# Expert weights by halves of the contraction, one queue for all loads, and a hinted jump

## The reference, cut to what matters

```python
for e in range(N_EXPERTS):
    h = jax.nn.silu(t @ w1[e]) * (t @ w3[e])
    y = y + combine[:, e:e + 1] * (h @ w2[e])
```

## Time and profile before

| | |
|---|---|
| median of the runs | 752.1 us |
| the profiled execution's own time | 756.08 us |
| its span, first to last instruction | 753.9 us |
| TensorE busy (matmul) | 665.2 us, 88% |
| VectorE, ScalarE busy | 220.6 us, 171.4 us |
| mean granted TensorE clock | 0.948 |
| read from HBM | 228.23 MB, 304 GB/s over the span |
| first MoE stage, pair 0 to pair 7 | 144.5 to 366.5 us |
| second MoE stage | 519.9 to 741.8 us |

### The profile page before, as it was taken

The page is one execution under the profiler, slowest core; times in us unless marked ns, Lnnn a source line. Parts: engine busy times, 40 slices in busy tenths (PEclk is TensorE's granted clock), DMA queues, the critical chain, the costliest instruction groups (busy, mean ns, idle before and its releaser), DMA issues.

```text
span 753.9 us, 7800 instructions
## 1 busy us (share of the span) xinstructions
PE 665.2 (88%) x2948; PEld 293.7 (39%) x2948; DVE 220.6 (29%) x628; ACT 171.4 (23%) x380; POOL 17.9 (2%) x29
## 2 busy tenths in 40 slices
PE   5997999899999979995589877999999999799864
PEld 2444544533434323331144444455343343243221
DVE  2367812420222110210224588124202220112102
ACT  2015712212220220210401366022112202202101
POOL 2000000000000000000001021000000000000000
PEclk9997999999999998998979979997999999989988
DMA  9999534489999999999999346642999999999951
GB/s 275 276 280 394 203 109 166 177 325 399 392 396 391 398 395 392 399 389 397 295 263 333 142 105 206 228 177 109 360 399 393 396 392 396 397 389 399 391 207 57
DMA packets 94392, 229.70 MB, mean 305 GB/s; under 512 B 2363, under 2 KB 2443, under 8 KB 94364
## 3 DMA queue, kind: packets, MB, share of 16 engines
q1 hardware_dynamic: 85184, 195.08, 72.4%
q10 hardware_dynamic: 7612, 29.74, 10.0%
q0 software_dynamic: 1568, 4.50, 2.5%
HBM read 228.23 MB, written 1.08 MB: 304 GB/s over the span
## 4 chain that ended last, share of the span: by engine, by line
DMA 44%; PE 43%; DVE 7%; issue 3%; ACT 1%; SPq 1%; DVEq 0%; ACTq 0%
DMA attw<-in_w_dram 23%; DMA ring<-in_w_dram 19%; PE ps L881 11%; PE ps L1044 9%; PE ps L954 7%; PE ps L1068 5%; PE ps L1014 2%; PE ps L1025 2%; DMA attw<-in_w_qkv_dram 2%; PE ps L918 1%; PE ps L932 1%; DVE attw L641 1%; PE ps L945 1%; DVE attw L626 1%; PE ps L996 1%
## 5 line engine op out<-in xcount | busy, mean ns | idle before, releaser
L1044 PE MATMUL ps<-attw,work 128*64 128x512 f32 x512 | 120.5, 628 | 28.8 <-DMA attw<-in_w_dram 28.8
L1068 PE MATMUL ps<-ring,work 128*64 128x512 f32 x384 | 114.3, 595 | 2.9 <-ACT work L485 2.9
L1044 PE MATMUL ps<-ring,work 128*64 128x512 f32 x512 | 111.6, 594 | 0.0
L881 PE MATMUL ps<-attw,work 128*128 128x512 f32 x192 | 87.1, 614 | 0.5 <-DMA attw<-in_w_qkv_dram 0.5
L757 DVE TENSOR_TENSOR work<-work,ps 128x512 f32<-128x512 f32 x16 | 11.0, 688 | 249.8 <-PE ps L1044 249.8
L1044 PEld LDWEIGHTS ps<-attw,work 128*64 128x64 f32 x512 | 40.6, 145 | 107.6 <-issue 107.6
L494 ACT COPY work<-ps 32x512 f32<-32x512 f32 x64 | 36.9, 577 | 132.0 <-PE ps L1068 131.5
L1044 PEld LDWEIGHTS ps<-ring,work 128*64 128x64 f32 x512 | 37.8, 137 | 67.8 <-issue 66.8
L766 DVE COPY work<-ps 32x512 f32<-32x512 f32 x64 | 43.9, 686 | 59.9 <-PE ps L1068 59.3
L1068 PE MATMUL ps<-attw,work 128*64 128x512 f32 x128 | 57.6, 595 | 0.6 <-ACT work L485 0.6
L954 PE MATMUL ps<-attw,work 128*128 128x512 f32 x128 | 56.3, 595 | 0.0
(11 more groups left out here) (133 smaller groups left out, 483.2 us busy)
## 6 DMA issues: line engine op xcount, KB each, us to landing
ring<-in_w_dram SPq DMA_DIRECT2D x42, 2048.0 KB, 16.7
attw<-in_w_dram SPq DMA_DIRECT2D x40, 2048.0 KB, 16.0
ring<-in_w_dram ACTq DMA_DIRECT2D x14, 2048.0 KB, 12.6
attw<-in_w_qkv_dram SPq DMA_DIRECT2D x4, 2048.0 KB, 16.7
attw<-in_w_o_dram SPq DMA_DIRECT2D x8, 1024.0 KB, 20.6
attw<-in_w_qkv_dram SPq DMA_DIRECT2D x4, 1024.0 KB, 15.0
attw<-bias_rows POOLq DMA_DIRECT2D x8, 256.0 KB, 3.6
x_sb<-in_x_dram SPq DMA_DIRECT2D x2, 512.0 KB, 5.9
```

What stands on the lines that cost most here:

```text
L881: last = pe.matmul(ps[:, g, :], xT[:, k, P * tt:P * tt + P], wqkv[part][:, k, :], start=(k == 0), stop=(k == KB - 1))
L1044: last = pe.matmul(ps[64 * e:64 * e + 64, 6 + which, :], xg[:, k, c:c + 2 * SLOTS], w13(which, e)[:, k, :], start=(k == 0), stop=(k == KB ...
L1068: last = pe.matmul(ps[64 * e:64 * e + 64, 4 + half, :], hT[:, k, 64 * e:64 * e + 64], w2(e)[:, k, 512 * half:512 * half + 512], start=(k = ...
```

## The change

A unit now is a half of the contraction of one matrix for both experts of a pair (blocks 0 to 3 and 4 to 7 of w1 and w3, 0 and 1, 2 and 3 of w2), loaded by two DMAs of 1 MB, one for each expert. TensorE waits for a unit where its half begins and signals behind each half (`w13_used` counts four a pair). w2 runs half by half of the contraction: both halves of the columns with unit 4, and then both with unit 5; `w2_used` now counts three a pair, one behind unit 4 and one behind each half of columns with unit 5. The waits for landings in `load_over` are gone. Unit 5 of pair i+1 is issued by SP, behind unit 4 of pair i+2. TensorE reads the flag ahead of the last pair, and its branch over the extra rounds is hinted from there. The other engines jump as before.

```diff
-        def ring_w13(which, e):
-            return ring[:, 2 * which + e, :].rearrange("p (k f) -> p k f", k=KB)
+        def w13_view(unit):
+            return unit.rearrange("p (e k f) -> p e k f", e=2, k=KB // 2)
+        def w2_view(unit):
+            return unit.rearrange("p (e k f) -> p e k f", e=2, k=FB // 2)
+        def ring_w13(which, kh):
+            return w13_view(ring[:, 2 * which + kh, :])
...
-        w1v = w1.rearrange("l e (k p) f -> l e p k f", p=P)
+        w1v = w1.rearrange("l (q e) (h k p) f -> l q h e p k f", e=2, h=2, p=P)
...
-                sp.dma_start(dst, view[L, 2 * pair + u % 2]).then_inc(landed, 16)
+                for e in range(2):
+                    sp.dma_start(dst[:, e], view[L, pair, u % 2, e]).then_inc(landed, 16)
...
-            def load_over(L, i, load_pair, mine, others, done, others_done):
-                n = PAIRS * L + i + 1
-                sp.wait_ge(main.w1_used, n)
+            def load_over(L, i, load_pair):
+                n = PAIRS * L + i
+                sp.wait_ge(main.w13_used, 4 * n + 1)
                 load_pair(L, i + 2, (0,))
-                sp.wait_ge(others[4], others_done)
+                sp.wait_ge(main.w13_used, 4 * n + 2)
                 load_pair(L, i + 2, (1,))
-                sp.wait_ge(main.w3_used, n)
+                sp.wait_ge(main.w13_used, 4 * n + 3)
                 load_pair(L, i + 2, (2,))
-                sp.wait_ge(mine[1], done)
+                sp.wait_ge(main.w13_used, 4 * n + 4)
                 load_pair(L, i + 2, (3,))
-                sp.wait_ge(main.w2_used, 2 * n)
+                sp.wait_ge(main.w2_used, 3 * n + 1)
                 load_pair(L, i + 2, (4,))
+                sp.wait_ge(main.w2_used, 3 * n + 3)
+                load_unit(L, i + 1, 5, last_landed)
...
+                sp.wait_ge(main.w2_used, 3 * (n - 1))
+                load_unit(L, PAIRS - 1, 5, last_landed)
                 if L + 1 < DEPTH:
-                    sp.wait_ge(main.w1_used, n)
+                    sp.wait_ge(main.w13_used, 4 * n - 3)
                     load_wqkv(L + 1, 0)
+                    sp.wait_ge(main.w13_used, 4 * n - 2)
                     load_wqkv(L + 1, 1)
-                    sp.wait_ge(main.w3_used, n)
+                    sp.wait_ge(main.w13_used, 4 * n - 1)
                     load_wqkv(L + 1, 2)
-                    load_wo(L + 1, 0)
-                    sp.wait_ge(main.w2_used, 2 * n)
-                    load_wo(L + 1, 1)
+                    sp.wait_ge(main.w13_used, 4 * n)
+                    sp.wait_ge(main.w2_used, 3 * n - 2)
+                    for a in range(2):
+                        load_wo(L + 1, a)
...
-                    if load_last:
-                        act.dma_start(ring_w2(1), w2v[L, 2 * (i + 1) + 1]).then_inc(last_landed, 16)
...
-                    landed(4)
-                    landed(5)
-                    for half in range(2):
-                        for k in range(FB):
+                    def down(kh, half):
+                        for k in range(2 * kh, 2 * kh + 2):
...
+                    landed(4)
+                    down(0, 0)
+                    pe.wait_ge(m.pct_copied, n + 1)
+                    down(0, 1).then_inc(m.w2_used, 1)
+                    if fetch:
+                        gather(m, 1, 6)
+                        pe.wait_ge(m.xg_copied, QUARTERS * G + QUARTERS + 1)
+                        gather(m, 2, 7)
+                    landed(5)
+                    for half in range(2):
+                        down(1, half).then_inc(m.w2_used, 1)
...
+                def look_ahead():
+                    ahead["more"] = more_rounds(pe, L)
+                    ahead["hint"] = pe.mark_branch_hint_location()
+
+                moe_round(main, L, GROUPS * L + 1, even_has, odd_has, odd_w13, odd_w2, before_last=look_ahead)
                 scatter(main, PAIRS * (L + 1), final=True)
-                with pe.If(more_rounds(pe, L)):
+                only_pe = [mybir.EngineType.PE]
+                extra_name, after_name = f"extra_rounds{L}", f"after_rounds{L}"
+                pe.br_lt(ahead["more"], 1, on_true=after_name, on_false=extra_name).branch_hint(ahead["hint"])
+                with nc.body(extra_name, valid_engines=only_pe):
```

More of the change, by code:

```diff
@@ L116, in encoder, with ring_w2, odd_w13, odd_w2 @@
         rope_raw = consts[:, o:TABLE].rearrange("p (w t a s) -> p w t a s", w=2, t=TT, a=2)
-        def ring_w13(which, e):
-            return ring[:, 2 * which + e, :].rearrange("p (k f) -> p k f", k=KB)
-        def ring_w2(e):
-            return ring[:, 4 + e, :].rearrange("p (k f) -> p k f", k=FB)
+        def w13_view(unit):
[4 more added lines that the diff above has]
+            return w13_view(ring[:, 2 * which + kh, :])
+        def ring_w2(kh):
+            return w2_view(ring[:, 4 + kh, :])
         wqkv = [attw[:, u, :].rearrange("p (k f) -> p k f", k=KB) for u in range(3)]
         wo = attw[:, 3:5, :].rearrange("p u f -> p (u f)").rearrange("p (b f) -> p b f", b=KB)
[L128 to L132, removed]
+        def odd_w13(which, kh):
+            return w13_view(attw[:, 2 * which + kh, :])
+        def odd_w2(kh):
+            return ring_w2(1) if kh else w2_view(attw[:, 4, :])
         vv = attw[:, 0, 0:512].rearrange("p (t c) -> p t c", t=TT)
@@ L230, in encoder @@
         first_banks = (6, 7, 5, 4)
-        w1v = w1.rearrange("l e (k p) f -> l e p k f", p=P)
-        w3v = w3.rearrange("l e (k p) f -> l e p k f", p=P)
-        w2v = w2.rearrange("l e (k p) f -> l e p k f", p=P)
+        w1v = w1.rearrange("l (q e) (h k p) f -> l q h e p k f", e=2, h=2, p=P)
+        w3v = w3.rearrange("l (q e) (h k p) f -> l q h e p k f", e=2, h=2, p=P)
+        w2v = w2.rearrange("l (q e) (h k p) f -> l q h e p k f", e=2, h=2, p=P)
         def more_rounds(eng, L):
             eng.wait_ge(flag_ready, L + 1)
-            return eng.value_load(flag[0:1, L:L + 1], min_val=0, max_val=1) > 0
+            return eng.value_load(flag[0:1, L:L + 1], min_val=0, max_val=1)
         block = ctx.enter_context(nc.Block())
@@ L478, in _, with moe_pair @@
                         act.activation(rt[9][:, 0:TT], rt[9][:, 0:TT], ACT.Exp).then_inc(exp_out, 1)
-                def moe_pair(m, R, i, load_last=False):
+                def moe_pair(m, R, i):
                     n = PAIRS * R + i
-                    act.wait_ge(m.w1_used, n + 1)
+                    act.wait_ge(m.w13_used, 4 * n + 2)
                     act.activation(h_sb, ps[:, 6, :], ACT.Silu).then_inc(m.silu_done, 1)
@@ L495, in moe_pair @@
                     last.then_inc(m.y1_copied, 1)
[L497 to L500, removed]
+                with act.Fori(0, PAIRS) as i:
+                    moe_pair(main, L, i)
+                with act.If(more_rounds(act, L) > 0):
                     with act.Fori(0, ROUNDS - 1) as r:
@@ L755, in moe_pair @@
                 dve.wait_ge(m.silu_done, n + 1)
[L756 removed]
+                dve.wait_ge(m.w13_used, 4 * n + 4)
                 dve.tensor_tensor(h_sb, h_sb, ps[:, 7, :], ALU.mult).then_inc(m.h_ready, 1)
@@ L761, in moe_pair @@
                     copy_gathered(L, m, G + 1, 2, 7)
-                dve.wait_ge(m.w2_used, 2 * n + 1 + m.credit)
+                dve.wait_ge(m.w2_used, 3 * n + 2 + m.credit)
                 for tt in range(TT):
@@ L817, in _ @@
                 moe_round(L, main, L, L == 0)
-                with dve.If(more_rounds(dve, L)):
+                with dve.If(more_rounds(dve, L) > 0):
                     m = extra[L]
@@ L1034, in moe_pair @@
                     fetch = j and not last_pair
-                    for which, used in ((0, m.w1_used), (1, m.w3_used)):
-                        landed(2 * which)
-                        landed(2 * which + 1)
+                    for which in range(2):
                         for k in range(KB):
+                            if k % 4 == 0:
+                                landed(2 * which + k // 4)
                             if not j and not which and k in (0, 6):
@@ L1044, in moe_pair @@
                                 last = pe.matmul(ps[64 * e:64 * e + 64, 6 + which, :],
-                                                 xg[:, k, c:c + 2 * SLOTS], w13(which, e)[:, k, :],
+                                                 xg[:, k, c:c + 2 * SLOTS], w13(which, k // 4)[:, e, k % 4, :],
                                                  start=(k == 0), stop=(k == KB - 1), tile_position=(0, 64 * e))
-                        last.then_inc(used, 1)
+                            if k % 4 == 3:
+                                last.then_inc(m.w13_used, 1)
                     if not first:
@@ L1069, in moe_pair @@
                                                  hT[:, k, 64 * e:64 * e + 64],
-                                                 w2(e)[:, k, 512 * half:512 * half + 512],
+                                                 w2(kh)[:, e, k % 2, 512 * half:512 * half + 512],
```

(9 more changed lines are left out.)

26 lines of the change are left out of this document (12 added, 14 removed).

## The result

The changed kernel took 762.2 us (median of 18 runs, 759.7 to 768.4) against 753.3 us of the kernel before in as many (751.6 to 759.9): 9.0 us more, a ratio of 1.0127 with a 95% interval of 1.0103 to 1.0151. It is slower. The forecast was 758.9 us in a range of 753.5 to 768.5, and 6.8 us more than before; the direction and the place were right, the gain of the hinted jump did not come.

The account below looks back on a forecast made before the run. Each MoE stage was taken as bound by a never-pausing load stream plus TensorE work behind its last landing that matters. +8.0 + 8.0 - 6.84 - 2.4 = +6.8 us on 752.1 gave 758.9 us, range 753.5 to 768.5.

Parts of the forecast that it names:

- The earlier start: First load of each MoE stage goes out after half of w1's use, at 148.3 instead of 151.8 us: 3.5 us sooner.
- The new order: Unit 5 lands behind the next pair's units 0 to 4; TensorE waits in w2; each MoE stage 8.0 us longer.
- The 36 units: Loads moving before pair 6's unit 5 lands: 195.9 us with both latencies, from 148.3 to 344.2 us.
- The tail: TensorE work behind pair 6's unit 5: half of w2 3.6, pair 7 24.1, clock 2.6; last w2 matmul at 374.5 us.
- the clock: Half clock on TensorE after the last wait for unit 5: 2.6 us more, ends 0 and 2.6.
- The halves' transfers: Two 1 MB DMAs per unit, 96 more issues over both layers: 0 us, range -3 to +3 a stage.
- Rival D: The halves slow the load stream by 1.5%: +3 us a stage, total 764.9 us; chance 0.10.
- Finer waits: Two more waits and two more semaphore steps a pair on TensorE: no cost.
- The jump: Hinted TensorE branch behind the first MoE stage: stall gone, -6.84 us once, and -2.4 us of half clock.
- Rival B: Hint does nothing, TensorE still sits some 7 us in the branch: total 768.1 us; chance 0.15.
- Rival C: Unit 5 is not late in w2; each stage gains 3.5 us and the jump 9.2: total 735.9 us; chance 0.08.

Follow-up runs that it names:

- experiment 2: Kernel before, with only unit 5 of pair i+1 issued by SP behind unit 4 of pair i+2 instead of by ScalarE: 780.6 us, ratio 1.0352.
- experiment 1: Changed kernel with unit 5 issued again by ScalarE from its own queue, the rest kept: 735.0 us, ratio 0.9754.
- experiment 3: Changed kernel with unit 5 of pair i+1 issued one unit earlier, behind unit 3 of pair i+2: 756.1 us, ratio 1.0026.
- experiment 4: Changed kernel with unit 5 of pair i+1 issued behind unit 1 of pair i+2 instead of unit 4: 747.4 us, ratio 0.9937.
- experiment 9: Changed kernel with only TensorE's loop over pairs placed at instruction 128 of a 16 KB code block: 758.6 us, ratio 1.0070.
- experiment 5: Changed kernel with TensorE's branch hint marked ahead of pair 0 instead of the last pair: 762.9 us, ratio 1.0120.
- experiment 7: Kernel of experiment 1 with TensorE's loop over pairs placed at instruction 0 of a 16 KB code block: 738.8 us, ratio 0.9789.
- experiment 8: Kernel of experiment 1 with TensorE's loop over pairs placed at instruction 128 of a 16 KB code block: 730.5 us, ratio 0.9671.
- experiment 6: Changed kernel with no branch hint, the flag still read ahead of the last pair: 766.9 us, ratio 1.0150.

## Why the prediction was right, step by step

**The earlier start** was sized rightly. The first load went out 3.85 us into the stage instead of 7.29, 3.44 us sooner; 3.5 were forecast.

**The new order** is what made the change slower, as forecast: experiment 2 has it alone (+13.8 us a stage), experiment 1 takes it away (-14.8), experiments 3 and 4 shift it place by place. Unit 5 of pair 6 landed 341.08 - 141.78 = 199.3 us into the stage; 344.2 - 144.5 = 199.7 were forecast. The 36 units that move before it are thus a sound way to time it. Of the four waits forecast at 4 to 6 us, three took 4.70 to 5.36 and one 2.55.

The experiments also separate the order from the halves. The new order costs 13.8 us a stage with whole matrices (experiment 2 against the kernel before) and 14.8 with halves (the changed kernel against experiment 1). The halves, with SP's waits for landings gone, gain 8.0 us a stage in the old order (experiment 1) and 7.1 in the new one (235.7 to 228.6).

**The tail** behind it was forecast as 3.6 + 24.1 + 2.6 = 30.3 us and took 29.3. The term that was off is the clock: 5.30 instead of 3.6 us for the half of w2, 1.7 and not 2.6. It varies: the four waits above were followed by 5.36, 6.46, 5.35 and 5.30 us. With 0.4 us of the landing these make 228.6 instead of 230 us, 6.8 a stage instead of 8.0.

**The halves' transfers** cost nothing, as taken. Rival D (a slower stream) is out: the changed kernel moved 393 GB/s from 155 to 340 us and experiment 1 395 from 155 to 345, against 394 before.

**Finer waits** cost nothing: w2's blocks without a wait take 3.60 and 3.65 us, half of 7.09.

**The jump** is the step that failed. I counted -6.84 and -2.4 us; in the changed kernel the stall is 5.85 us, and 16 transposes and 64 matmuls took 3.57 and 27.46 instead of 3.67 and 28.45. That is 1.0 + 1.1 = 2.1 us, not 9.2, none of it shown to be the hint's. Rival B named what happened, with a chance of 0.15; its 768.1 was too high since it had the stages 2.5 us too long and nothing for the 3.8 us that the passage got shorter. What spoils the hint is not the queues' load alone: with the same loads in flight the place of the code decided, which nothing in the profile of before could show. Experiment 9 has what I had summed up: from the end of w2 to the end of the 64 matmuls it takes 407.02 - 371.39 = 35.6 us, where the kernel before took 411.23 - 366.46 = 44.8, 9.2 less, as forecast. Its whole passage is 8.0 shorter, 145.4 instead of 153.5, and it took 758.6 us, beside the 758.9 predicted. That agreement is closer than its parts: in that kernel the stages are 1.6 us shorter than in my sum and the passage 1.2 longer, and the median of the kernel before was 752.1 to 754.3 us from one set of runs to the other.

In the changed kernel itself two errors pull against each other. The stages cost 2.5 us less than forecast (13.5 instead of 16.0), and the passage gained 5.4 less (3.8 instead of 9.2). That the total is only 3.3 us off is in part luck.

The passage of the changed kernel is 3.8 us shorter though the stall went by 1.0 only. One further piece is in layer 1's router, where half clock was granted for 10.2 us before and for 3.4 after:

```profile
507.50:517.70 10.20, 9.38 (x32) 6.96 (x32) 5.07 (x31) 4.02 (x5) 0.00 (x0) 0.50 0.65 257
```

```profile
511.70:515.10 3.40, 3.16 (x7) 1.07 (x5) 3.02 (x23) 0.79 (x1) 0.00 (x0) 0.50 1.03 424
```

This is not the whole of it, since in the attention ahead of the router half clock lasted 3.4 us longer than before. From the end of the 64 matmuls to the next stage half clock was granted for 23.9 us before, 20.5 in the changed kernel and 27.3 in experiment 9, and that stretch took 108.7, 107.0 and 109.8 us. Why it differs, I did not try; the change doesn't touch that part.

**Rival C** (unit 5 in time) is what experiment 1 built, and its 735.9 lies near the 735.0 measured, but by luck: it had 3.5 us for each stage and 9.2 for the jump, where experiment 1 gained 8.0 in each stage and its branch still took 7037 ns in layer 0. The case for it in "DMA: Bandwidth & Descriptors" of the Trainium skill, that issuing from several engines only saves the issuers' time, does not hold for the order of service: experiment 2 moved one load of six from one queue to the other and lost 3.5%. By the rule on queues served in turn, on the same page of the Trainium skill, ScalarE's loads would go beside SP's; experiment 1 agrees, where they landed 8.3 to 14.7 us after their issue, beside a full stream.

## What to carry to other kernels

In a load stream that never pauses, count the transfers ahead of the one that is waited for last and then the work behind that wait; both stand in the trace of before, and a buffer without a double must not queue behind loads that are needed later. Cutting loads and work into halves, with the waits for landings dropped, gained 7.1 to 8.0 us a stage here in either order of the loads; an order that is not that of their use cost 13.8 to 14.8, more than the halves gave. A hinted jump is to be checked at the branch itself, in each place where it is made: the same hint brought 4 to 6 us in layer 0 at one place in the code (145.4 us between the stages against 149.7 and 151.2), and at another none that a trace shows.

## What the runs showed of the hardware that was not expected

TensorE's hinted branch was short or long with the same hint, by the place of the code: in layer 0 it took 6.9 to 9.2 us in six kernels (the changed one and experiments 1, 3, 4, 5 and 7) and 355 and 358 ns in two (8 and 9), in layer 1 342 to 363 ns in seven and 3443 ns in one (7). Where it was short, a 16 KB code fetch had started behind both the hint and the end of TensorE's loop, and ahead of the branch; where it was long there was none in that stretch, and one started 1 to 6 us into the branch. A fetch in that stretch is not enough by itself: experiment 6, without a hint, has one in both layers (at 345.9 and 726.9 us), and both its branches are long. The profile doesn't say which code a fetch brings. What decides whether the hint's fetch is made I have not settled; marking the hint 200 us earlier did not do it.

Each wait of 2.5 to 5.4 us in the changed kernel's w2 was followed, in the first stage, by a stretch at half clock that cost 1.7 to 2.8 us, even the shortest; in the second stage the four waits, of 3.9 to 5.4 us, cost 1.4 to 2.5. The length of the wait alone doesn't settle it: TensorE stands still for 2.53 us ahead of the last scatter too, and its 8 matmuls then took 1.99 us in the changed kernel's first stage and 3.56, at half clock, in experiment 8's. Ahead of a further wait for a landing this costs nothing, since the waits still ended 31.9 us apart; behind the last wait it counts in full.
